# Modulations taken from the middle of a recurrence and put at five stage borders, and a table's transfers issued four at a time

## The reference, cut to what matters

```python
for i in range(DEPTH):                                   # 2 layers
    ml = jnp.split(s_lat @ w_ada[i] + b_ada[i], 6, axis=-1)   # w_ada[i]: 1024 x 6144
    mc = jnp.split(s_ctx @ w_ada[i] + b_ada[i], 6, axis=-1)
    u_lat = modulate(h_lat, g_pre_mix[i], ml[0], ml[1])       # parts 0 and 1, at the layer's start
    ...                                                       # layer 0: a recurrence and attention
    h_lat = h_lat + ml[2] * rms_norm(o_lat, g_post_mix[i])    # part 2, after the mixer
    f_lat = sqrelu_mlp(modulate(h_lat, g_pre_ff[i], ml[3], ml[4]), w_ff1[i], w_ff2[i])
    h_lat = h_lat + ml[5] * rms_norm(f_lat, g_post_ff[i])     # part 5, after the feed-forward
```

```python
bias = rpb[:, dr[:, None, None, :, None], dc[None, :, :, None, :]]
s_lat = s_lat + bias.transpose(1, 2, 0, 3, 4, 5).astype(jnp.float32)
```

## Time and profile before

| | |
|---|---|
| three runs | 2100.88, 2102.44, 2102.47 us; median 2102.44 |
| the profiled execution | 2100.61 us, of it 2098.8 between the first and the last instruction (the span) |
| busy in the span | PE 1863.1 us (89%), DVE 1109.6 (53%), ACT 886.5 (42%), POOL 214.4 (10%) |
| mean granted clock of PE | 0.948 of full speed |
| start and projections | 0 to 246 us |
| recurrence's preparation, units, last chain | 246 to 270, 270 to 652, 652 to 686 us |
| mix0, its border | 672 to 721, 721 to 742 us |
| feed-forward of layer 0, its border | 742 to 1098, 1098 to 1124 us |
| odd layer's attention and its projections | 1124 to about 1290 us |

### The profile page before, as it was taken

The page is one execution under the profiler, slowest core; times in us unless marked ns, Lnnn a source line. Parts: engine busy times, 40 slices in busy tenths (PEclk is TensorE's granted clock), DMA queues, the critical chain, the costliest instruction groups (busy, mean ns, idle before and its releaser), DMA issues.

```text
span 2098.8 us, 40122 instructions
## 1 busy us (share of the span) xinstructions
PE 1863.1 (89%) x16962; PEld 1558.0 (74%) x16962; DVE 1109.6 (53%) x1711; ACT 886.5 (42%) x1423; POOL 214.4 (10%) x214
## 2 busy tenths in 40 slices
PE   5899779888898889999997799799979999679996
PEld 3776568777787688888876676698877677569985
DVE  1457564565545554224344765565445574556863
ACT  2336544353431444214224256564332465346652
POOL 0000035334342000000000100010000000000210
PEclk9999889999999999999998899899989999789998
DMA  8233232222231312233323310365534534134552
GB/s 268 92 121 109 77 121 85 87 91 91 83 103 42 121 61 92 90 100 101 101 80 58 133 61 25 103 186 190 186 108 148 169 98 151 65 124 161 181 163 99
DMA packets 201377, 237.19 MB, mean 113 GB/s; under 512 B 14347, under 2 KB 158573, under 8 KB 201197
## 3 DMA queue, kind: packets, MB, share of 16 engines
q1 hardware_dynamic: 195856, 227.33, 34.2%
q10 hardware_dynamic: 5341, 7.30, 1.0%
HBM read 233.56 MB, written 1.05 MB: 112 GB/s over the span
## 4 chain that ended last, share of the span: by engine, by line
PE 75%; DVE 10%; ACT 6%; issue 2%; POOL 2%; SPq 2%; DMA 2%; ACTq 0%; DVEq 0%; POOLq 0%
PE bank L1377 17%; PE bank L1378 17%; PE bank L1379 17%; PE bank L1569 9%; ACT window L2448 2%; SPq L2896 2%; DVE window L1869 2%; PE bank L1557 2%; PE bank L1536 2%; PE bank L1548 2%; PE bank L1428 1%; PE bank L1442 1%; DVE window L1920 1%; PE bank L1754 1%; PE bank L1576 1%
## 5 line engine op out<-in xcount | busy, mean ns | idle before, releaser
L1377 PE MATMUL bank<-window 128*128 128x512 f32 (+1 forms) x2136 | 762.8, 357 | 55.1 <-DVE window L1920 29.6
L1378 PE MATMUL bank<-window 128*128 128x512 f32 (+1 forms) x2136 | 749.8, 351 | 0.0
L1379 PE MATMUL bank<-window 128*128 128x512 f32 (+1 forms) x2136 | 749.0, 351 | 0.0
L1869 DVE TENSOR_TENSOR window<-arena,window 128x2048 fp32r<-128x2048 f32 (+1 forms) x164 | 372.1, 2269 | 271.5 <-ACT window L2448 269.7
L1377 PEld LDWEIGHTS bank<-window 128*128 128x128 f32 x2136 | 415.5, 195 | 119.0 <-DVE window L1920 30.7
L2448 ACT ACTIVATE window<-arena 128x2048 fp32r<-128x2048 f32 (+3 forms) x292 | 377.1, 1291 | 211.0 <-PE bank L1379 123.5
L1379 PEld LDWEIGHTS bank<-window 128*128 128x128 f32 x2136 | 415.2, 194 | 51.3
L1378 PEld LDWEIGHTS bank<-window 128*128 128x128 f32 x2136 | 416.0, 195 | 48.2 <-issue 0.2
L2448 ACT ACTIVATE arena<-bank 128x256 f32<-128x256 f32 (+1 forms) x298 | 127.0, 426 | 367.1 <-PE bank L1379 128.6
L1569 PE MATMUL bank<-arena 64*64 64x64 f32 (+1 forms) x5888 | 215.2, 228 | 18.8 <-DVE arena L1363 10.2
L1569 PEld LDWEIGHTS bank<-arena 64*64 64x64 f32 x5888 | 201.8, 137 | 35.6 <-DVE arena L1363 11.9
(11 more groups left out here) (283 smaller groups left out, 1674.8 us busy)
## 6 DMA issues: line engine op xcount, KB each, us to landing
arena<-in_w_ff SPq DMA_DIRECT2D x64, 1024.0 KB, 5.4
arena<-in_w_ada SPq DMA_DIRECT2D x48, 1024.0 KB, 5.6
arena<-in_w_in SPq DMA_DIRECT2D x23, 1024.0 KB, 5.1
arena<-in_w_ffn_up SPq DMA_DIRECT2D x22, 1024.0 KB, 5.0
arena<-in_w_ffn_down SPq DMA_DIRECT2D x10, 1024.0 KB, 5.1
arena<-in_w_in_even SPq DMA_DIRECT2D x9, 1024.0 KB, 5.5
arena<-in_w_out SPq DMA_DIRECT2D x8, 1024.0 KB, 5.2
arena<-in_w_in_odd SPq DMA_DIRECT2D x8, 1024.0 KB, 6.9
```

The costliest lines, as they stand in the source:

```text
L1377: e.matmul(o, rr(l[0]), rr(r[0]), start=start, stop=False)
L1378: e.matmul(o, rr(l[0]), rr(r[1]), start=False, stop=False)
L1379: return e.matmul(o, rr(l[1]), rr(r[0]), start=False, stop=stop)
L1869: e.tensor_tensor(rr(raw), raw, rr(w.high, F32), SUB).then_inc(*ve.tick(w.ready))
```

## The change

Five edits in one.

1. `modulation` becomes a case of `modulations(which)`, which takes any list of slices; the row buffer of a slice goes by its place in the order of all slices and not by its number.
2. The recurrence's rounds keep 12 slices: (1, 4..7) and (1, 12..19), one in two rounds, the turn of a slice now in the round of the next slice.
3. Twenty slices move: (0, 16..19) between the steps of `prepare(0)`, ahead of the lanes; (1, 0..3) beside `chain(3)` behind the last unit; (0, 20..23) behind the last block of `mix0`, (1, 8..11) behind that of `ff0`, and (1, 20..23) behind that of `mix1`, where `out_proj` advances them in turn with the tiles that are still on their way.
4. Loads move with them: each slice's 1 MB takes the ring's next slot at its new place, ahead of the chunks that follow there.
5. The position table's transfers are issued four at a time, one group behind each of the eight steps of the vC projection, and so behind the load of vC's first chunk.

```diff
+    def modulations(which):
+        prev = None
+        for now in which:
+            mod(*now)
+            if prev is not None:
+                turn_row(*prev)
+            prev = now
+            yield
+        turn_row(*prev)
+        yield
...
-        while going:
+        meanwhile = list(meanwhile)
+        while going or meanwhile:
+            meanwhile = advance(meanwhile)
             going = advance(going)
...
     now = prepare(0)
+    filling = modulation(0, 16, 20)
     while (0, 0) not in prepared:
         next(now)
-    left = iter([(0, i) for i in range(16, 24)] + [(1, i) for i in range(24)])
-
-    def conditions():
-        for i, f in left:
-            mod(i, f)
-            yield
-            turn_row(i, f)
-            yield
+        next(filling, None)
+    for _ in filling:
+        pass
...
-    run(*[lane(n, work) for n in range(LANES)], preparing(now), chaining(), conditions())
+    run(*[lane(n, work) for n in range(LANES)], preparing(now), chaining(), slowed(modulations([(1, s) for s in (4, 5, 6, 7, *range(12, 20))])))
...
-    run(*pending, others(), slowed(gate_rows_(0, 2, 2, stage("units"))))
+    run(*pending, others(), slowed(gate_rows_(0, 2, 2, stage("units"))), modulation(1, 0, 4))
...
-             then=[normed("f0", k, True) for k in range(4)])
+             then=[normed("f0", k, True) for k in range(4)], meanwhile=[modulation(0, 20, 24)])
...
-    step("load bias")
-
     c_done = []
+    bias_loads = iter(range(0, len(bias_pairs), 4))
...
                 step("vC", y, k)
                 if y:
                     give("vC", k)
+                step("load bias", next(bias_loads))
                 yield
...
-        def load_bias():
+        def load_bias(n):
             sp.wait_ge(*stage("ff0"))
-            load(landed_bias, at("bias"), bias_pairs)
+            load(landed_bias, at("bias"), bias_pairs[n:n + 4])
```

More of the change, by code:

```diff
@@ L379, in turn_row @@
         give("turn", i, s)
-    def modulation(i, f0=0, f1=24):
[L382 to L387, removed]
-            yield
-        turn_row(i, prev)
+    def modulations(which):
[8 more added lines that the diff above has]
+        yield
+    def modulation(i, f0=0, f1=24):
+        yield from modulations([(i, s) for s in range(f0, f1)])
     norms = {}
@@ L448, in fours, with out_proj @@
         return [(W, k0 + k, x0 + k, min(4, nk - k)) for k in range(0, nk, 4)]
-    def out_proj(name, parts, x, ntok, O, points=(), ready=None, add=False, gate=False, then=()):
+    def out_proj(name, parts, x, ntok, O, points=(), ready=None, add=False, gate=False, then=(), meanwhile=()):
         outs[name] = Out(parts, x, ntok, O, points, ready, add, gate, then)
@@ L919, in program, with ffn @@
     ffs = {}
-    def ffn(i, ntok, xr, T, norm_gain, norm_shift, points):
+    def ffn(i, ntok, xr, T, norm_gain, norm_shift, points, meanwhile=()):
         n = ntok * 128
@@ L957, in ffn @@
             out_proj(("ff2", i, part), parts, F.h1, ntok, F.O, (), {j: [at("ff1 part", i, part, j)] for j in range(nt)},
-                     part > 0, end, then=[normed(T, k, True) for k in range(ntok)] if end else ())
+                     part > 0, end, then=[normed(T, k, True) for k in range(ntok)] if end else (), meanwhile=meanwhile if end else ())
         return x_ready(T, range(ntok))
-    xr = ffn(0, 4, xr, "m1", lambda f, s: DER[:, 2, f, s:s + 1], lambda f, s: MOD[1][:, f, s:s + 1], [*stage("mix0")])
+    xr = ffn(0, 4, xr, "m1", lambda f, s: DER[:, 2, f, s:s + 1], lambda f, s: MOD[1][:, f, s:s + 1], [*stage("mix0")], [modulation(1, 8, 12)])
     norms["m1"].made = [at("gain", 2)]
@@ L1093, in program @@
     out_proj("mix1", fours(I["w_out"][1], 0, 8), OP_o, 2, O_o, (), {k: [at("part o odd", k // 2 * 2)] for k in range(8)}, gate=True,
-             then=[normed("f1", k, True) for k in range(2)])
+             then=[normed("f1", k, True) for k in range(2)], meanwhile=[modulation(1, 20, 24)])
     xr = x_ready("f1", range(2))
@@ L1431, in turn @@
         def turn(i, s):
-            u, a = bank("turn", i, s), arow[s % 2]
+            u, a = bank("turn", i, s), arow[order_of_mod.index((i, s)) % 2]
             pe.wait_ge(at("arow", i, s), u.before)
@@ L2472, in mod @@
             sc.wait_ge(sc.last(), u.full, *([at("turned", *order_of_mod[n - 2])] if n > 1 else []))
-            copy(arow[s % 2], u.b[:, 0:256]).then_inc(*sc.tick(u.empty, at("arow", i, s)))
+            copy(arow[n % 2], u.b[:, 0:256]).then_inc(*sc.tick(u.empty, at("arow", i, s)))
         def split(key):
```

## The result

| | before | changed |
|---|---|---|
| runs, us | 2100.88 to 2102.47 (4) | 2113.03, 2115.30, 2116.97, 2120.92 |
| median | 2102.43 | **2116.14** |
| profiled execution, its span | 2100.61, 2098.8 | 2116.97, 2115.2 |
| mean granted clock | 0.948 | 0.940 |

The ratio is 1.0069, with a 95% interval of 1.0049 to 1.0089: the change costs 13.7 us. The forecast was 2108.5 (+6), with a range from 2092 to 2117.

The account below looks back on a forecast made before the run. PE was taken to bound most of the recurrence (busy 232.8 of 258 us), ACT and DVE the borders. -17 + 17.5 + 3.5 + 17 - 15 = +6 on 2100.61, plus 1.8 for the median, gave 2108.5 us, range 2092 to 2117.

Parts of the forecast that it names:

- The sign: Whole kernel: the change was forecast to be slower, by 0.3%, with a chance of 0.5 for slower.
- A: Recurrence: twenty modulations leave PE's queue, saving at most the 18.1 us on the chain of waits; -17, ends -9 and -33.
- B: Start: four slices that wait for loads stand ahead of lora on PE and delay the first units; +17.5, ends +14 and +20.
- D: Three borders, four slices each: the next weights' split lands inside the border on ACT and DVE; +17, ends +4 and +22.
- the forecast's own case: Whole kernel: a time from 2103 to 2113 us, given a chance of 0.38.
- rival 4: Recurrence: the other engines' chains close in, so the gain stays at -9; total +14, 2116.5 us; chance 0.12.
- E: Position table, four transfers at a time: PE's waits of 13.8 us around vC's weights nearly vanish; -15, ends -10 and -16.
- C: Last chain steps: four slices' loads delay the first w_out chunk, whose split holds up DVE's chain steps; +3.5, ends 0 and +6.
- Rival 1: Recurrence bound by PE throughout, so the moved modulations save 33 us there; total -10, 2092.5 us; chance 0.2.
- Rival 2: Borders: work in PE's gaps keeps the clock up, 3.4 us at each of three; total -4, 2098.5 us; chance 0.1.
- Rival 3: Borders: the weights' splits are hidden and only the copies cost, +4; total -7, 2095.5 us; chance 0.12.
- rival 5: Position table: POOL's mask additions meet a DVE operation, so the gain is -11, not -15; total +10, 2112.5 us; chance 0.08.

Follow-up runs that it names:

- experiments 7 and 8: Kernel before with two slices at each of mix0's and ff0's borders, the next stage's first chunk loaded behind them (2105.26 us) or ahead (2105.59 us).
- Experiment 3: Kernel before with only slices (0, 16..19) moved into the start, placed behind the lora step of the first preparation: 2105.54 us, ratio 1.0015.
- experiment 5: Kernel before with only slices (1, 0..3) moved beside the last chain, 28 staying in the recurrence: 2101.42 us, ratio 1.0001.
- E, no mask: Kernel before with only the position table issued four at a time, and POOL's two mask additions cut to 16 columns each: 2086.99 us, ratio 0.9940.
- E alone: Kernel before with only the position table's transfers issued four at a time, all modulations staying in the recurrence: 2090.38 us, ratio 0.9949.
- experiment 10: Kernel before with the table issued four at a time and POOL's mask in eight additions of two heads: 2089.92 us, ratio 0.9958.
- experiments 1, 2, 4, 5: Kernel before with, respectively, only the four-at-a-time table, start slices, twelve border slices, or last-chain slices changed: 2090.38, 2116.70, 2105.71, 2101.42 us.

## Why the prediction was right, and where its sizes were off

The sign and the range held, and so did steps A, B and D. The range held by luck: the median came 7.6 us above the forecast, outside the forecast's own case (2103 to 2113) and 0.9 below the end of the range, and that end was worked out from rival 4, which did not come. In the profiled execution the span grew by 16.4, 10.4 more than the sum of +6: E is short by 8.1 and C by 3.9, the other three by 1.0 together, and 2.6 came back in the stretches that I had at nothing.

**A, right (-17; measured -17.5, and -16.7 and -13.1 in the two other kernels that move all twenty).** The chain's 18.1 was the better guide than the 33.0 of PE's busy time. Rival 1, for which A was -33, is refuted by the same stretch. The gain for each slice that leaves is 0.6 to 0.7 us at four slices (experiments 7 and 8, with four slices fewer in the recurrence too, show 0.9 and 1.1), 0.74 at twelve, 0.80 at sixteen and 0.66 to 0.88 at twenty, where PE worked 1.65 for each; with single executions that differ by up to 4.4 us, no rise with the number is shown. The other half is in the windows: 8.1 us more idle time and a lower clock. Rival 4, which had these chains close in entirely, did not come.

**B, right (+17.5; +18.7), by its mechanism.** Experiment 3 changes PE's order and gets 11 of 15 us back. Of the clock the step had too little: L1654 starts 18.7 us late, where order and loads made 16.5, so 2.2 stand against the 1 that was added.

**C, mis-sized (+3.5; +7.4).** The third megabyte was to come near 662.5 and came at 664.97, since SP issued it at 655.19 behind two more modulation loads; the chain's end moved by 4.9, not 3.5. The other 2.5 stands where the clock was at half behind waits, of which the step had nothing. It is no fixed price of that wait: in experiment 5 the same 4.9 of chain came with +1.8 and -1.8 (C is +4.9 there), while the four profiled kernels that have the border slices too all show +7.4. Why they differ stays open.

**D, right in sum (+17; +17.3), and in the place it named.** Experiments 7 and 8 show it: the split behind the slices costs 5, ahead of them 1 and 0.3. At mix1 the price was 8.0 and not 6.5 (6.7 to 8.2 in the other profiled kernels with four slices there). Rival 2 fell as the step had it: the slices fill the border's early gaps at a clock of 1.00, and the stop of 5 us comes last, so the product behind it starts at 0.50. The Trainium skill ("TensorE: Matmul & The Clock Gate", HAM oscillation) says to leave PE no long idle gaps; the windows show that a fill which ends before the last wait gives nothing back. Rival 3, hidden splits, holds only where the split goes first, and the change does not do that.

**E, mis-sized (-15; -6.9).** The step "one thing comes late: POOL's mask additions" was priced at nothing in the sum, and it is the one that failed. They meet three DVE products, which I had named as rival 5 with a chance of 0.08 and +4 us. Without the mask E gives 13.6, near the forecast; with it 9.4 alone and 6.9 in the changed kernel. The times in us between the starts of some PE instructions show where it went (lines as in the kernel before):

| from, to | before | E, no mask | E alone | changed |
|---|---|---|---|---|
| ff0's border to vC | 41.9 | 27.7 | 27.7 | 30.4 |
| to L1518, which reads the norm products | 17.8 | 19.9 | 19.9 | 15.5 |
| to L1525 | 4.1 | 4.1 | 8.4 | 11.0 |
| to the scores | 24.8 | 23.3 | 23.3 | 24.8 |

The third row is the mask's: it costs 4.2 in E alone, which is rival 5's price, and 6.9 in the changed kernel, if that kernel without its mask would take the 4.1 too (no run has it). There PE waits 3.86 and then works for 4 us at 0.50, and for some 4 us more below full speed. Counted from the border, the additions start at the same place in both kernels (40.5 and 40.6 us), but DVE's three products start at 43.0 in the changed kernel and at 44.3 in E alone, so more of them lies beside the additions, 7.82 for 6.68. The earlier products go with a wait that is missing: in E alone PE waits 2.46 us ahead of L1738, whose result DVE needs for them, and works at 0.57 behind it (1159 to 1163); the changed kernel does not wait there.

The other rows come to -0.2 together: +2.7 from the wait of 2.65 for a chunk's split behind the border and the clock of 0.60 after it, which belong to the modulations at that border; -4.4 where the wait ahead of L1738 (L1731 before) and the slow clock behind it are missing; and +1.5 at a clock of 0.70 and 0.87 ahead of the scores, where E alone has 1.00. So theory 2 of experiment 1 has a part in it: the border does take 2.7 us of E's gain, but the second row gives more than that back.

The Trainium skill ("SBUF — State Buffer", Terms) says that the loser of the port pair is blocked for the whole instruction. The traces agree: three products took 6.68 and 7.82 us beside the additions and 1.79 without them, and 3.73 when the additions were cut into eight. The operations that were not blocked read one tensor from SBUF only: the reciprocals (6.93 with the mask and without it) and L2001, which reads a bank, 0.42.

**The sum.** By their medians the four parts alone (experiments 1, 2, 4, 5) make -11.3 + 15.0 + 4.1 - 0.1 = +7.7, and the change is +13.7. Their intervals (2.8, 2.6, 1.8 and 1.9 us, and 4.2 for the change; together some 6.3) just allow a difference of 6. In the profiled executions the spans make -8.6 + 19.1 + 4.6 + 1.8 = +16.9 and the change +16.4. So nothing shows that the parts work on one another by more than these runs can tell in the total. In its own stretch E is worth less in company in each trace (-6.9 and -7.1 against -9.4); whether that holds for the total stays open.

## What to carry to other kernels

Work that is moved into idle time of one engine is paid by the queues: here every place had room on PE. At the start the price was PE's own queue, where the first units stood behind four slices that waited for loads; at the borders and beside the last chain it was the weights' split that now stood behind a load, on ACT and DVE. Ask of each moved step which operation of the *next* stage it is put ahead of, and put that one first. A full engine is worth what the chain of waits says and not its busy time: here half. And when a wait is taken away, look at what now runs beside what: the four-at-a-time table alone took 2090.38 us, half a per cent less than the kernel before (with the mask in pieces 2089.92, which the intervals do not tell from it), and it still left 4 us to a mask that came at the wrong moment.

## What the runs showed of the hardware

- A wait costs more than its length. In the changed kernel PE stood for 2.21, 3.46 and 3.86 us (ahead of 670.16, 693.96 and 1192.34), and behind each a window of 4 us in which PE was busy all the time shows a granted clock of 0.50 to 0.53, near the lower of its two levels (1.2 GHz). Around the mask this cost 1.8 us on top of the wait of 2.43 in E alone and 3.0 on top of 3.86 in the changed kernel. Ahead of L1738 a wait of 2.46 in E alone was followed by 0.57 and one of 1.76 in experiment 10 by 1.00.
- Eight POOL additions of a quarter of the size took 13.2 us and two whole ones 9.6, both beside DVE's norm products and what follows them: cutting an instruction that blocks lets the other engine in between but made the total longer here.
- SP took 10.6 to 14.7 us for sixteen table transfers of 64 KB, where 32 took 21.7 in one block before.
- The recurrence, untouched in its order, differed by 0.9 to 2.1 us between profiled executions of three kernels, and by up to 4.4 between three that share the change's order: one profile is no measure of a microsecond there.
